# Attention steps with gates: the second bank of transposes goes from VectorE to ScalarE

## The chip, the cores and the metric

The kernel runs on one core of one Trainium2 chip. The metric is the device time of one execution in microseconds (us), lower is better. The engines meant below are TensorE (PE, with its weight loads PEld), VectorE (DVE), ScalarE (ACT), GpSimd (POOL) and SyncE (SP).

## The reference

Two transformer blocks in float32 work on 512 tokens of width 1024. The first block is a SwiGLU layer, a mixing layer and another SwiGLU layer; the second has a chunked attention, a latent attention and two convolutional SwiGLU layers. The change sits in the mixing layer of the first block. Its heads come in two kinds of eight. The first kind is attention over a band of 128 tokens with a sink. The second kind adds up three attentions, each scaled by a gate of its own:

```
o_cmp, o_sel = nsa_cmp_sel(q_b, k_c, v_c, k_s, v_s, tbl_b)
o_win = banded_attention(q_b, k_w, v_w, tbl_b, WINDOW_B, None)
o_b = gates[:, :, 0] * o_cmp + gates[:, :, 1] * o_sel + gates[:, :, 2] * o_win
```

With 512 tokens all eight blocks of 64 are selected, and a window of 512 covers everything, so that o_sel and o_win are both plain causal attentions over all tokens, with different keys and values. o_cmp attends to 31 compressed keys.

## The kernel before

**Groups and steps.** The mixing layer's attention is one object, att_1, of class PairAttention. It works on two heads at a time. First come 8 steps of the banded kind (four groups of two, given a sink). Then come four groups of the mixed kind, numbered 0 to 3 here, of five steps each. Steps A and B are o_sel and steps C and D are o_win: A and C handle the token blocks 3 and 0, B and D the blocks 2 and 1, each for two heads, so a step has four units. Step W handles the compressed keys. A, B, C and D are given a gate. The units of A and C are 512, 512, 128 and 128 keys wide, those of B and D 384, 384, 256 and 256. This makes 16 steps with a gate.

**What one step needs.** TensorE makes the scores (L1810). VectorE adds the bias and takes the row minimum, one instruction per unit (L1974). ScalarE takes the exponential with its row sum, one per unit (L1906). VectorE inverts the sums, of units 0 and 1 at L1948 and of units 2 and 3 at L1961. The probabilities are scaled by inverse and gate (L2033), unit 0 on VectorE and the others on GpSimd. TensorE transposes them in tiles of 128x128 (L1832) into up to three PSUM banks: the first holds unit 0, the second unit 1, and the third units 2 and 3, which is 512, 512 and 256 columns for A and C and 384, 384 and 512 for B and D. The banks are copied into score in SBUF, by ScalarE at L1919 or by VectorE at L1921. TensorE multiplies them with the values (L1857), units 0 and 1 first, and units 2 and 3 as soon as the third bank is copied. When a group's last step is through, ScalarE and VectorE take the result out (L1894, L1899).

**Order by hand.** Every engine has its own order, written as a loop over k, the step whose scores are made. With lag 2, the pass of the loop for step k also handles step k-2's transposes and copies, and step k-3's values. Within mixed groups the pass for A copies the D before, B copies W, C copies A, D copies B, and W copies C. TensorE's pass is scores of k, values of k-3, transposes of k-2. ScalarE's pass is in the function act below. VectorE's pass, beyond what is printed at the end of this section, is in short:

```
self.biased_dve(dve, k)
...
dve.wait_ge(self.e, self.after("e", k, 2))
dve.reciprocal(self.inverses(k, 0, 2), self.sums(k, 0, 2)).then_inc(self.r, 1)
...
self.copies(dve, copied, "dve")
...
self.scaled_dve(dve, k, 1)
...
dve.wait_ge(self.e, self.after("e", k))
```

The last wait is for all four exponentials of step k; the second inversion follows, and then the next pass begins with biased_dve of step k+1. For W the pass is different: L1990 to L1997 prepare it, ScalarE takes its exponential last in its own pass (L1890), and VectorE then takes its sums (L2002 to L2006). In groups 1 and 2 VectorE also splits half a chunk of a later weight in that pass (L2345). After W of group 3 there are no more scores, and TensorE fills the passes with pieces of the output projection (L351 to L353).

Of the kernel before, what the change touches and what calls it, by code (L numbers as in the profile page):

```python
# [87 lines left out]
def program(nc, A, strips_dram, skewed, rows_dram, out):  # L88
    stack = ExitStack()
    with stack:  # L90
# [229 lines left out]
        def split_hi(act, c, slot, land, n=CHUNK):  # L320
            act.wait_ge(raw_landed[slot], land)
            if not isinstance(c, int) or c > 3:
                act.wait_ge(used, c - 2)
            act.activation(w_hi[:, slot, :n], raw[:, slot, :n], ACT.Copy).then_inc(hi_done, 1)  # L324
# [190 lines left out]
        def root_table(act):  # L515

            act.wait_ge(lo_done, 2)
            act.activation(stat[:, 0:1], eps[:, :], ACT.Sqrt)

        def c_row_act(act):  # L520
            act.wait_ge(cond_in, 16)
            act.activation(c_row[:, :], c_row[:, :], ACT.Silu).then_inc(cond_done, 1)
# [56 lines left out]
        class Norm:  # L579
            parts = 1  # L580

            def __init__(self, ready, gains=None, shifts=None, first=0, again=False, tile=xn_tile, banks=None):
                self.tile = tile
                self.n, self.ready, self.gains, self.shifts, self.again = TOK * norms[0], ready, gains, shifts, again
                norms[0] += 1
                self.root_n = TOK * roots[0]
                if not again:
                    roots[0] += 1
                self.first = first
                self.banks = banks or [bank[(t + first) % KT] for t in range(KT)]  # L590
                if gains is not None:
                    self.t, self.e = transposed[0], evacuated[0]
                    transposed[0] += KT
                    evacuated[0] += self.parts * KT
                if shifts is not None:
                    self.f = shifted[0]
                    shifted[0] += self.parts * KT // 2
# [16 lines left out]
            def act(self, act, gained=None, between=None):  # L614

                if not self.again:
                    for s in range(TOK):
                        self.stats_act(act, s)
                if between:
                    between(act)  # L620
                if gained is not None:
                    act.wait_ge(*gained)
                self.evacuate_act(act, range(KT))
# [1062 lines left out]
        class Step:  # L1686


            def __init__(self, units, sink=None, gate=None):
                self.units, self.sink, self.gate, self.windows = units, sink, gate, None  # L1690
                self.banks, width = [], SEQ + 1
                for i, unit in enumerate(units):
                    if width + unit.n > SEQ:
                        self.banks.append([])
                        width = 0
                    unit.bank, unit.col = len(self.banks) - 1, width
                    self.banks[-1].append(i)
                    width += unit.n
                self.copies = ["act", "dve", "act"][:len(self.banks)]
                self.by_dve = [i for i in range(4) if i in SCALED_BY_DVE]  # L1700
                self.by_pool = [i for i in range(4) if i not in SCALED_BY_DVE]
                self.counts = dict(s=4, b=4, e=4, r=2 if sink is None else 1, n=len(self.by_pool), nd=len(self.by_dve), t=len(self.banks),
                                   pa=self.copies.count("act"), pd=self.copies.count("dve"), o=2)
# [4 lines left out]
        class Windows:  # L1708


            def __init__(self, p):
                self.windows, self.sink, self.copies = p, None, ["act"]
                self.counts = dict(s=2, b=1, e=1, r=1, n=1, nd=0, t=1, pa=1, pd=0, o=2)

        pair_link = Count(sem("pair_link"))
# [1 line left out]
        class PairAttention:  # L1717
# [146 lines left out]
            def act(self, act, beside={}):  # L1864
                lag = self.lag
                for k in range(len(self.steps) + lag + 1):
                    if k in beside:
                        beside[k](act)
                    step = self.steps[k] if k < len(self.steps) else None
                    out_of, copied = k - lag - 1, k - lag  # L1870
                    early = out_of in self.last and self.steps[out_of].windows is not None
                    if early:
                        self.out_act(act, out_of)
                    if step and step.windows is None:
                        self.exps_act(act, k, (0, 1))
                    if out_of in self.last and not early:
                        self.out_act(act, out_of)
                    if 0 <= copied < len(self.steps):
                        self.copies(act, copied, "act", (0,))
                    if step and step.windows is None:  # L1880
                        self.exps_act(act, k, (2, 3))
                    if step and step.sink is not None:
                        act.wait_ge(self.sink_d, self.sinks_to(k))
                        at = 16 + 4 * (k % 2)
                        act.activation(stat[:, at:at + 4], stat[:, at:at + 4], ACT.Exp).then_inc(self.sink_e, 1)
                    if 0 <= copied < len(self.steps):
                        self.copies(act, copied, "act", (1, 2))
                    if step and step.windows is not None:
                        act.wait_ge(self.apart, self.windows_to(k))
                        act.activation(self.window_probs(k), self.window_probs(k), ACT.Exp, scale=-1.0).then_inc(self.e, 1)  # L1890
# [1336 lines left out]
```

## Time and profile before

| | |
|---|---|
| median of 3 runs | 2224.39 us (2224.09 to 2224.95) |
| profiled execution, its own time | 2223.66 us |
| span of the profiled execution | 2222.1 us |
| busy: PE, PEld | 2176.4 us (98%), 1816.4 us (82%) |
| busy: DVE, ACT, POOL | 1275.6 us (57%), 898.9 us (40%), 267.4 us (12%) |
| mixed groups, first bias to last values of W | 523.3 to 612.3 us of the span |

Busy time is the time in which an engine executed instructions. The granted clock is the share of TensorE's full speed that it was allowed. In a timeline, a row has its start in us from the beginning of the span, its length, the engine, the line of the kernel, the operation and its tiles, and in brackets how long the engine sat idle before it and who ended that. Consecutive rows overlap a little, because an instruction starts before the one ahead of it has left the engine.

### The profile page before, as it was taken

The page shows a single profiled execution, that of the slowest core. Times are in us where ns is not written, and L with a number is a line of the kernel's source. Part 1 is how long each engine was busy: PE and PEld are TensorE (multiplying, and loading weights), DVE is VectorE, ACT ScalarE, POOL GpSimd, SP SyncE. Part 2 cuts the span into 40 slices and gives each one's busy share as a digit, 9 for nine tenths or more (in the row PEclk, how much of TensorE's full clock was granted, in tenths as well). Part 3 has the DMA queues.
Part 4 walks back from the last instruction along what each step waited for, and adds up shares of the span by engine and source line. Part 5 has one row for each costly group of instructions (what it writes and reads, how often), then busy time and mean ns, then how long its engine had stood idle before and what let it go on. Part 6 is the DMA issues. An engine that isn't in the chain of part 4 may idle for free.

```text
span 2222.1 us, 30869 instructions
## 1 busy us (share of the span) xinstructions
PE 2176.4 (98%) x11681; PEld 1816.4 (82%) x11681; DVE 1275.6 (57%) x2136; ACT 898.9 (40%) x1492; POOL 267.4 (12%) x445
## 2 busy tenths in 40 slices
PE   7999999998999999999999999999999999999998
PEld 6888888877888888888888888888878788888887
DVE  5764764557753363365347766456476766555654
ACT  4222223456642222225237544234264745432343
POOL 2110220045300020010027000000000430000000
PEclk9999999999999999999999999999999999999999
DMA  8864993231034284274231342332313112323332
GB/s 263 285 207 125 320 304 103 95 88 39 30 114 114 76 273 142 66 246 143 95 105 41 91 110 79 105 100 80 114 50 102 61 48 80 100 86 104 94 93 96
DMA packets 260212, 270.42 MB, mean 122 GB/s; under 512 B 9190, under 2 KB 202365, under 8 KB 260109
## 3 DMA queue, kind: packets, MB, share of 16 engines
q1 hardware_dynamic: 238381, 190.40, 28.8%
q0 software_dynamic: 21728, 78.63, 10.2%
q8 instruction: 66, 1.08, 0.2%
q14 instruction: 37, 0.30, 0.0%
HBM read 265.72 MB, written 12.72 MB: 125 GB/s over the span
## 4 chain that ended last, share of the span: by engine, by line
PE 85%; DVE 6%; ACT 5%; issue 1%; POOL 1%; DMA 1%; SPq 0%; DVEq 0%; ACTq 0%; POOLq 0%
PE bank L345 16%; PE bank L346 16%; PE bank L347 15%; PE bank L351 11%; PE bank L353 11%; PE bank L352 11%; PE bank L1857 2%; PE bank L1832 2%; PE bank L1810 2%; ACT probs L1906 1%; DVE w_lo L328 1%; ACT w_hi L324 1%; POOL probs L2032 1%; DVE probs L1974 1%; ACT xT_hi L773 1%
## 5 line engine op out<-in xcount | busy, mean ns | idle before, releaser
L345 PE MATMUL bank<-xT_hi,w_hi 128*128 128x512 f32 (+1 forms) x1624 | 620.3, 382 | 7.0 <-DVE xT_lo L789 2.3
L346 PE MATMUL bank<-xT_lo,w_hi 128*128 128x512 f32 (+1 forms) x1624 | 618.3, 381 | 0.0
L347 PE MATMUL bank<-xT_hi,w_lo 128*128 128x512 f32 (+1 forms) x1624 | 618.2, 381 | 0.0
L328 DVE TENSOR_TENSOR w_lo<-raw,w_hi 128x2048 fp32r<-128x2048 f32 (+2 forms) x200 | 411.0, 2055 | 316.8 <-ACT w_hi L324 315.1
L324 ACT ACTIVATE w_hi<-raw 128x2048 fp32r<-128x2048 f32 (+3 forms) x201 | 345.9, 1721 | 453.5 <-PE bank L353 396.2
L345 PEld LDWEIGHTS bank<-xT_hi,w_hi 128*128 128x128 f32 x1624 | 304.6, 188 | 69.1 <-DVE w_lo L328 5.4
L347 PEld LDWEIGHTS bank<-xT_hi,w_lo 128*128 128x128 f32 x1624 | 304.6, 188 | 59.2
L346 PEld LDWEIGHTS bank<-xT_lo,w_hi 128*128 128x128 f32 x1624 | 304.6, 188 | 58.0
L351 PE MATMUL bank<-w_hi,hid_hi 128*128 128x512 f32 x704 | 274.1, 389 | 0.0
L353 PE MATMUL bank<-w_hi,hid_lo 128*128 128x512 f32 x704 | 273.9, 389 | 0.0
L352 PE MATMUL bank<-w_lo,hid_hi 128*128 128x512 f32 x704 | 273.9, 389 | 0.0
L2032 POOL TENSOR_SCALAR probs<-probs,small 128x256 f32<-128x256 f32 (+2 forms) x120 | 113.8, 960 | 692.4 <-DVE small L1948 673.5
L1027 ACT ACTIVATE hid_hi<-act_u 128x512 f32 (+1 forms) x88 | 55.6, 632 | 310.2 <-DVE act_u L1103 310.2
L353 PEld LDWEIGHTS bank<-w_hi,hid_lo 128*128 128x128 f32 x704 | 132.2, 188 | 27.7
L351 PEld LDWEIGHTS bank<-w_hi,hid_hi 128*128 128x128 f32 x704 | 132.2, 188 | 27.2
L352 PEld LDWEIGHTS bank<-w_lo,hid_hi 128*128 128x128 f32 x704 | 132.2, 188 | 27.2
L1906 ACT ACTIVATE probs<-probs,small 128x512 f32<-128x512 f32 (+2 forms) x224 | 120.8, 542 | 48.8 <-DVE small L1974 48.8
L1095 DVE SCALAR_TENSOR_TENSOR act_u<-bank,cols,act_u 128x511 f32<-128x511 f32 x88 | 65.9, 749 | 94.1 <-ACT act_u L1019 89.0
L1019 ACT ACTIVATE act_u<-bank,cols 128x512 f32<-128x512 f32 x44 | 34.3, 780 | 178.2 <-PE bank L347 178.2
L351 PE MATMUL bank<-w_hi,xT_hi 128*128 128x512 f32 (+2 forms) x288 | 101.8, 354 | 3.3 <-DVE xT_lo L789 2.4
L1106 DVE TENSOR_TENSOR hid_lo<-act_u,hid_hi 128x512 f32 (+1 forms) x88 | 60.9, 693 | 75.4 <-ACT hid_hi L1027 75.4
L352 PE MATMUL bank<-w_lo,xT_hi 128*128 128x512 f32 (+2 forms) x288 | 100.1, 348 | 0.0
(330 smaller groups left out, 2754.6 us busy)
## 6 DMA issues: line engine op xcount, KB each, us to landing
raw<-in_ffn_w_in_dram SPq DMA_DIRECT2D x40, 1024.0 KB, 6.2
raw<-in_f_win_dram SPq DMA_DIRECT2D x40, 1024.0 KB, 6.0
mod_w<-in_mod_w_dram POOLq DMA_DIRECT2D x48, 512.0 KB, 5.9
mod_w_more<-in_mod_w_dram POOLq DMA_DIRECT2D x48, 512.0 KB, 6.1
raw<-in_ffn_w_out_dram SPq DMA_DIRECT2D x24, 768.0 KB, 4.6
raw<-in_f_wout_dram SPq DMA_DIRECT2D x24, 768.0 KB, 4.5
raw<-in_a_wqkv_dram SPq DMA_DIRECT2D x12, 1024.0 KB, 5.1
skewed_strips<-bias_strips POOLq DMA_DIRECT2D x32, 320.0 KB, 6.8
```

What stands on the lines that cost most here:

```text
L324: act.activation(w_hi[:, slot, :n], raw[:, slot, :n], ACT.Copy).then_inc(hi_done, 1)
L328: dve.tensor_tensor(out=w_lo[:, slot, :n], in0=raw[:, slot, :n], in1=w_hi[:, slot, :n].bitcast(f32), op=ALU.subtract).then_inc(lo_done, 1)
L345: pe.matmul(o, lhsT=w[0], rhs=xs[0], start=first, stop=False)
L346: pe.matmul(o, lhsT=w[0], rhs=xs[1], start=False, stop=False)
L347: return pe.matmul(o, lhsT=w[1], rhs=xs[0], start=False, stop=last)
L351: pe.matmul(o, lhsT=xs[0], rhs=w[0], start=first, stop=False)
L352: pe.matmul(o, lhsT=xs[0], rhs=w[1], start=False, stop=False)
L353: return pe.matmul(o, lhsT=xs[1], rhs=w[0], start=False, stop=last)
L1095: dve.scalar_tensor_tensor(out=dst[:, u, shift:], in0=bank[b][:, :SEQ - shift], scalar=w, in1=dst[:, u, shift:], op0=ALU.mult, op1=ALU.add ...
L1106: dve.tensor_tensor(out=hid[1], in0=act_u[:, u, :], in1=hid[0].bitcast(f32), op=ALU.subtract).then_inc(pair_free[u], 1)
L1906: act.activation(p, p, ACT.Exp, scale=-1.0, bias=self.least(k, i), accum_out=self.sums(k, i)).then_inc(self.e, 1)
L2032: return engine.tensor_scalar(p, p, self.inverses(k, i), None, ALU.mult)
```

## The change

In steps that have a gate, the second bank (unit 1's) is copied by ScalarE directly behind the first one, and no longer by VectorE. The other steps are as before.

```
-                self.copies = ["act", "dve", "act"][:len(self.banks)]
+                self.copies = ["act", "dve" if gate is None else "act", "act"][:len(self.banks)]
...
-                self.windows, self.sink, self.copies = p, None, ["act"]
+                self.windows, self.sink, self.gate, self.copies = p, None, None, ["act"]
...
                     if 0 <= copied < len(self.steps):
-                        self.copies(act, copied, "act", (0,))
+                        self.copies(act, copied, "act", (0,) if self.steps[copied].gate is None else (0, 1))
...
                     if 0 <= copied < len(self.steps):
-                        self.copies(act, copied, "act", (1, 2))
+                        self.copies(act, copied, "act", (1, 2) if self.steps[copied].gate is None else (2,))
```

The function copied, by which TensorE waits for banks, reads the same list, so it now waits for ScalarE's count alone in these steps.

## Rows read from the trace of the kernel before

**Rows 1.** Copies out of PSUM, whole run: count, then nanoseconds min/median/max, and forms.

```profile
L1919 ACT ACTIVATE score<-bank x108: 360/573/599, 494.2 to 1807.3; 128x512 f32<-128x512 f32 x56, 128x256 f32<-128x256 f32 x28, 128x384 f32<-128x384 f32 x24
...
L1921 DVE COPY score<-bank x56: 418/614/693, 494.3 to 1806.8; 128x512 f32<-128x512 f32 x28, 128x384 f32<-128x384 f32 x24, 128x256 f32<-128x256 f32 x4
```

**Rows 2.** Group 2: us, busy PE, PEld, DVE, ACT, POOL (instructions), clock, DMA, GB/s.

```profile
563.89:582.17 18.28, 17.53 (x214) 14.86 (x210) 16.15 (x58) 13.66 (x43) 8.37 (x17) 1.00 0.03 3
```

**Rows 3.** Chain that ended last, 515 to 640 us, its shares by line.

```profile
by line: ACT probs L1906 14.3%; DVE probs L1974 8.8%; PE bank L351 8.6%; PE bank L352 8.2%; PE bank L1857 8.2%; PE bank L353 8.2%; PE bank L1832 7.0%; issue 5.3%; DVE score L1921 4.9%; PE bank L2146 4.7%; ACT w_hi L324 3.0%; DVE q_lo L1899 
```

**Rows 4.** Timeline of ScalarE in group 2.

```profile
564.76 0.72 ACT L1906 ACTIVATE probs<-probs,small 128x512 f32<-128x512 f32 x1 [1.78 <-DVE small L1974]
...
566.18 0.47 ACT L1919 ACTIVATE score<-bank 128x384 f32<-128x384 f32 x1
566.55 0.39 ACT L1906 ACTIVATE probs<-probs,small 128x128 f32<-128x128 f32 x1
...
567.33 0.57 ACT L1919 ACTIVATE score<-bank 128x512 f32<-128x512 f32 x1
...
571.24 0.60 ACT L1894 ACTIVATE q_hi<-bank 128x512 fp32r<-128x512 f32 x1 [0.42 <-PE bank L2155]
...
573.15 0.58 ACT L1919 ACTIVATE score<-bank 128x512 f32<-128x512 f32 x1
573.63 0.39 ACT L1906 ACTIVATE probs<-probs,small 128x128 f32<-128x128 f32 x1
...
574.30 0.19 ACT L1906 ACTIVATION_READ_ACCUMULATOR probs<-probs,small 128x1 f32 x1
...
577.82 0.58 ACT L1919 ACTIVATE score<-bank 128x512 f32<-128x512 f32 x1
580.01 1.04 ACT L1919 ACTIVATE score<-bank 128x512 f32<-128x512 f32 x2 [1.61 <-PE bank L1832]
580.95 0.41 ACT L1890 ACTIVATE probs<-probs 128x256 f32<-128x256 f32 x1
```

**Rows 5.** Timeline of VectorE in group 2.

```profile
574.53 0.17 DVE L1961 RECIPROCAL small<-stat 128x2 f32<-128x2 f32 x1
...
577.95 0.17 DVE L1961 RECIPROCAL small<-stat 128x2 f32<-128x2 f32 x1 [0.22 <-ACT probs L1906]
...
581.39 0.42 DVE L2002 TENSOR_REDUCE stat<-probs 128x8 f32<-128x256 f32 x1
```

**Rows 6.** Timeline of TensorE in group 2, the values.

```profile
567.09 1.52 PE L1857 MATMUL bank<-score,v_tok 128*64 128x128 f32 x20
...
574.15 1.31 PE L1857 MATMUL bank<-score,v_tok 128*64 128x128 f32 x20 [0.65 <-DVE score L1921]
...
578.08 1.31 PE L1857 MATMUL bank<-score,v_tok 128*64 128x128 f32 x20
```

**Rows 7.** Timeline of ScalarE, then TensorE, in group 0.

```profile
540.97 0.58 ACT L1919 ACTIVATE score<-bank 128x512 f32<-128x512 f32 x1
543.32 1.04 ACT L1919 ACTIVATE score<-bank 128x512 f32<-128x512 f32 x2 [1.78 <-PE bank L1832]
544.25 0.41 ACT L1890 ACTIVATE probs<-probs 128x256 f32<-128x256 f32 x1
...
541.38 1.31 PE L1857 MATMUL bank<-score,v_tok 128*64 128x128 f32 x20
```

**Rows 8.** Timeline of TensorE behind group 3's last scores.

```profile
601.63 1.31 PE L1857 MATMUL bank<-score,v_tok 128*64 128x128 f32 x20
```

**Rows 9.** Who waited for whom, 523 to 612 us: total, times, longest.

```profile
PE bank L1857 <- DVE score L1921: 2.0, 3, 0.7
```

**Rows 10.** Stretches of 4 us, columns as in the second group.

```profile
508.00:512.00 4.00, 2.93 (x30) 2.45 (x31) 3.47 (x13) 0.95 (x6) 2.43 (x3) 1.00 0.00 0
512.00:516.00 4.00, 3.82 (x34) 3.12 (x32) 3.13 (x16) 3.15 (x13) 2.55 (x4) 0.66 0.42 131
...
572.00:576.00 4.00, 3.35 (x42) 2.84 (x41) 4.00 (x18) 3.52 (x13) 1.86 (x4) 1.00 0.01 2
```

## The prediction, made before the changed kernel was run

> **What bounds the kernel now.** I read the page first: TensorE is busy 98% of the span, so nearly everywhere else a shift of the other engines is free. The question is whether it is free where the change works, between 523 and 612 us. Next I read the chain that ended last over that stretch [rows 3]. TensorE does not own it there: ScalarE's exponentials, VectorE's biases and VectorE's copy (L1921, 4.9%) are on it. Then one mixed group by itself [rows 2]. A group takes 18.28 us (group 1 takes the same to the hundredth). VectorE is busy 16.15 of it, ScalarE 13.66, and TensorE 17.53. So three engines are each near their limit, and the order within the passes decides. Last came the timelines of group 2, engine by engine [rows 4 to 6].
>
> The reader should see a loop there. A bias on VectorE releases the exponentials of units 0 and 1 on ScalarE (the 1.78 us of idle time in [rows 4] end so); a copy sits between them and the exponentials of units 2 and 3; these release VectorE's second inversion; only behind it does the next step's bias run. Whatever ScalarE does between the two pairs of exponentials lengthens this loop. VectorE's copy, in contrast, runs beside the second pair of exponentials: in the pass for C, ScalarE's last exponential, whose sum is read out until 574.49 [rows 4], is done when VectorE with its copy and its scaling is done too, and the second inversion starts at 574.53 [rows 5].
>
> **The change by parts.** *Removed from VectorE:* 16 copies, 8 of 512 columns and 8 of 384, out of the 56 in [rows 1]. Their median is 0.61 us, so 2.5 us a group. Most are hidden beside the exponentials, as just said, so I count no gain for them in the loop. One gain could be in the pass for C, where TensorE waits 0.65 us for VectorE's copy before the values [rows 6], three times in all [rows 9]. But ScalarE's copy 0 starts at 573.15 and the next instruction follows at 573.63 [rows 4]; a copy 1 started there takes 0.58 and ends at 574.21, when TensorE, at 574.15, had already begun behind VectorE's. No gain there either.
>
> *Added to ScalarE:* the same 16 copies. The price of one is how much later the next instruction starts: 0.48 us for 512 columns (573.15 to 573.63) and 0.37 for 384 (566.18 to 566.55) [rows 4]. Back to back they should cost the same. Fourteen of them are ahead of the point where TensorE becomes the only bound (7 of each width); the last two, of C and D of group 3, fall between pieces of the projection, where TensorE has no idle time ahead of the values [rows 8], and cost nothing. If that cover failed, they would cost 0.85 more.
>
> *What is late next,* for one full group that starts with ScalarE and VectorE late by s, times of group 2:
> 1. Pass A copies D, 384 columns: the second exponentials and the third copy are 0.37 later. TensorE already waits for this third copy: its values at 567.09 take 1.52 us and not 1.31 [rows 6]. Six tenths of these values (those of units 0 and 1; 0.74 us of 1.24, which is 1.31 less the overlap with the next row) come before that bank, so the rest started at 567.09 + 0.74 + 0.21 = 568.04, which is 0.71 behind the third copy's start at 567.33. I use this 0.71 again. TensorE is late by s + 0.37.
> 2. Pass B copies W and is unchanged. At its end ScalarE waits 0.42 for TensorE's values of W before L1894 [rows 4], so it takes over TensorE's lateness, s + 0.37.
> 3. Pass C copies A, 512 columns: + 0.48. The inversion at 574.53 had no slack on ScalarE's side. Late: s + 0.85.
> 4. Pass D copies B, 384 columns: + 0.37, and the inversion at 577.95 was already waiting for ScalarE [rows 5]. Late: s + 1.22. The third copy moves from 577.82 to 579.04 + s, and the values of units 2 and 3 can start at 579.75 + s. They would have started at 578.08 + 0.74 = 578.82 [rows 6]. TensorE is late by s + 0.93; a slack of 0.29 is used up.
> 5. Pass W copies C. Before, copy 0 at 580.01, then a wait for the last transpose, copy 2, and L1890 at 580.95, 0.94 later [rows 4]. Now three copies back to back, 0.48 + 0.48 + 0.37 = 1.33, so L1890 and with it L2002 [rows 5] and the next group's bias are 0.39 later than TensorE: s + 1.32.
>
> So a full group adds 1.32 us. Group 0 begins undisturbed at its pass C: 0.48 + 0.37 = 0.85; the third copy at 540.97 then releases the values at 542.53, against 541.38 + 0.74 = 542.12 [rows 7], so TensorE is late by 0.41; L1890 then by 0.41 + 0.40 = 0.81. Groups 1 and 2 add 1.32 each: 3.45. Group 3 counts only up to the values of B, 0.93: 4.38. From there on TensorE is busy with pieces of the projection, and nothing later is changed, so the lateness reaches the end.
>
> Bounds: a copy costs nothing if ScalarE's idle time takes it, and at most its whole length, 0.58 or 0.47, if back to back copies do not overlap: 7 x 0.58 + 7 x 0.47 = 7.4 us. I take the steps of 0.48 and 0.37, since a copy is followed like that by another instruction in [rows 4]. *Moved waits:* the copy's wait for the transposes now holds up ScalarE's second exponentials, but the transposes of k-2 ended long before, except in pass W, which is item 5. TensorE has one wait fewer per step, worth hundredths.
>
> The profiled execution would go from 2223.66 to 2228.04 us; the median of the runs lies 0.73 above it, which makes 2228.8.
>
> **A rule that speaks for the change.** By [rows 2] VectorE is the busier of the two. The Trainium skill (Perfetto Trace Analysis, Identifying the Most-Contended Engine) says to find the vector or scalar engine with the highest occupancy and optimize that one first. By that rule, relieving VectorE should help, as in the third rival below.
>
> **Rivals.**
> - *Everything on the path.* No slack is found: all 14 copies at their steps, 7 x 0.48 + 7 x 0.37 = 5.95 us, 2230.3. For it: the loop has very little idle time. Against: the slacks in items 4 and 5 are in the rows.
> - *The clock falls.* More idle time of TensorE in passes A and C takes its clock down. In [rows 10] a stretch with 2.93 us busy of 4 is followed by one at 0.66; the one with 3.35, which holds the gap at 574.15, kept 1.00. That gap grows from 0.65 to about 0.8, so I expect 3.1 to 3.2 in the worst stretch, between the two. A fall would cost 4 x 0.34 = 1.4 us, once in each of three groups 4.1: 2232.9. [...]
> - *VectorE's relief pays* (not slower). ScalarE has 4.6 us of idle time in a group [rows 2], and if its copy came early enough the three waits of [rows 9] vanish: 2224.4 - 2.0 = 2222.4. It needs ScalarE's copy 1 to end before about 573.4, and its copy 0 alone ends at 573.73. At the extreme the whole share of L1921 leaves the chain [rows 3], 4.9% of 125 us = 6.1: 2218.3.
> - *Partly absorbed.* ScalarE's waits for VectorE and TensorE take half of it, because VectorE, 2.5 us a group less busy, is back sooner: 0 to 2.5 us, middle 2225.7. Against: VectorE's passes end on ScalarE's last exponential, not on its own work.
>
> That the change does not take effect is excluded by the code: the list of copies rules both engines and TensorE's waits.
>
> **How the numbers follow.** A measurement of this kernel tells about 0.2%, 4.45 us, from no change; that line is at 2228.84, and my forecast is almost on it. Chances: the forecast (3.0 to 5.5 us, 2227.4 to 2229.9) 0.60, split evenly by the line; all on the path 0.12 and the clock 0.07, both slower; partly absorbed 0.14 and the small gain 0.04, both within; the large gain 0.03. So slower 0.49, within 0.48, faster 0.03. The range of 2225.3 to 2230.9 leaves out the gains, the clock and about a third of the absorbed case, 0.19.
>
> **What would show it.** L1919 has 124 instructions and L1921 40. A full group takes 19.6 us and not 18.28, with ScalarE busy about 15.7 and VectorE 13.7 in it. In pass C the second inversion waits for ScalarE by some 0.4 us. L1921 is gone from the chain and L1919 is in it. TensorE's values of B wait for L1919 in every group. The projection's piece behind group 3's transposes starts 4.4 us later. The prediction is wrong if a group's length is 18.5 or less (then VectorE's release found a way into the loop that I have missed), if the clock falls, or if stages behind 640 us change their lengths.

## The result and the profile after

The changed kernel took 2229.11 us, the median of 18 runs (2226.54 to 2231.33), against 2224.51 of the kernel before (18 runs beside them, 2222.23 to 2226.72): a ratio of 1.0020, with a 95% interval of 1.0013 to 1.0026. That is 4.6 us slower, just over the line of 0.2% that the text before put at 4.45 us. A second measurement gave 2229.28 against 2224.11, a ratio of 1.0023 (1.0013 to 1.0034). The forecast was 2228.8.

The profiled execution took 2229.2 us, with a span of 2227.7, 5.6 longer than before. I split this span by one marker that all kernels have, ScalarE's L1894, which takes a group's result out. From its start in group 0's pass C to its start behind group 3 is "the stretch". It was 612.37 - 535.82 = 76.55 us before and 616.02 - 535.40 = 80.62 after: 4.07 more. Ahead of it, where nothing is changed yet, the start lies 0.42 earlier, and behind it 1.95 were lost (2227.7 - 616.02 = 1611.68 against 1609.73).

First the copies, one line of the kernel each, over the whole changed run. The counts are those expected, 124 and 40, to be held against [rows 1].

```profile
L1919 ACT ACTIVATE score<-bank x124: 362/574/598, 493.8 to 1812.6; 128x512 f32<-128x512 f32 x64, 128x384 f32<-128x384 f32 x32, 128x256 f32<-128x256 f32 x28
...
L1921 DVE COPY score<-bank x40: 417/614/692, 493.9 to 1812.2; 128x512 f32<-128x512 f32 x20, 128x384 f32<-128x384 f32 x16, 128x256 f32<-128x256 f32 x4
```

Then group 2 as a stretch, with the columns of [rows 2], and two stretches of 4 us in it in which TensorE worked little; the second is the least of the group.

```profile
564.55:584.10 19.55, 18.04 (x212) 14.86 (x210) 14.09 (x53) 15.26 (x47) 9.11 (x17) 1.00 0.00 1
...
568.00:572.00 4.00, 3.33 (x40) 2.36 (x40) 2.99 (x12) 3.73 (x15) 2.31 (x4) 1.00 0.00 0
...
574.00:578.00 4.00, 3.23 (x40) 2.51 (x39) 2.92 (x15) 3.52 (x12) 1.92 (x3) 1.00 0.00 0
```

The group takes 19.55 us where it took 18.28. ScalarE is busier and VectorE less busy, as meant, and now ScalarE is the busier of the two. The clock stays whole.

The chain that ended last, from 515 to 640 us, against [rows 3]: VectorE's copy is gone, and ScalarE's exponentials have 22% where they had 14%, and its copies 13.5% where the lines shown did not have them.

```profile
by line: ACT probs L1906 22.2%; ACT score L1919 13.5%; PE bank L351 7.6%; PE bank L352 7.3%; PE bank L353 7.2%; issue 6.9%; PE bank L1857 5.7%; DVE probs L1974 5.0%; PE bank L2155 3.4%; PE bank L1832 3.4%; ACT w_hi L324 3.0%; PE bank L1810 
```

Now the timelines of group 2: ScalarE, then VectorE, then TensorE. Their rows answer to [rows 4 to 6].

```profile
566.21 0.72 ACT L1906 ACTIVATE probs<-probs,small 128x512 f32<-128x512 f32 x1 [1.68 <-DVE small L1974]
...
567.63 0.85 ACT L1919 ACTIVATE score<-bank 128x384 f32<-128x384 f32 x2
568.37 0.39 ACT L1906 ACTIVATE probs<-probs,small 128x128 f32<-128x128 f32 x1
...
573.07 0.60 ACT L1894 ACTIVATE q_hi<-bank 128x512 fp32r<-128x512 f32 x1 [0.51 <-PE bank L2155]
...
574.97 1.07 ACT L1919 ACTIVATE score<-bank 128x512 f32<-128x512 f32 x2
575.93 0.41 ACT L1906 ACTIVATE probs<-probs,small 128x128 f32<-128x128 f32 x1
...
580.50 0.58 ACT L1919 ACTIVATE score<-bank 128x512 f32<-128x512 f32 x1
...
582.41 1.36 ACT L1919 ACTIVATE score<-bank 128x512 f32<-128x512 f32 x3 [1.33 <-PE bank L1832]
583.64 0.43 ACT L1890 ACTIVATE probs<-probs 128x256 f32<-128x256 f32 x1
```

```profile
576.84 0.17 DVE L1961 RECIPROCAL small<-stat 128x2 f32<-128x2 f32 x1 [0.98 <-ACT probs L1906]
...
580.63 0.17 DVE L1961 RECIPROCAL small<-stat 128x2 f32<-128x2 f32 x1 [1.05 <-ACT probs L1906]
...
584.10 0.42 DVE L2002 TENSOR_REDUCE stat<-probs 128x8 f32<-128x256 f32 x1 [0.72 <-ACT probs L1890]
```

```profile
568.53 0.88 PE L1857 MATMUL bank<-score,v_tok 128*64 128x128 f32 x12 [0.30 <-ACT score L1919]
569.78 0.66 PE L1857 MATMUL bank<-score,v_tok 128*64 128x128 f32 x8 [0.37 <-ACT score L1919]
...
576.10 1.47 PE L1857 MATMUL bank<-score,v_tok 128*64 128x128 f32 x20 [0.77 <-ACT score L1919]
...
580.18 1.60 PE L1857 MATMUL bank<-score,v_tok 128*64 128x128 f32 x20
```

The reader should see three things. A pair of copies takes 0.74 us (567.63 to 568.37) or 0.96 (574.97 to 575.93), twice the step of one. VectorE now idles about 1 us ahead of each second inversion in passes C and D, until ScalarE's last exponential: it waits for the time that its copy took, and for ScalarE's delay on top. And TensorE waits for L1919 in pass C, where it waited for L1921, and in pass A, where no wait of its own stood ahead of these values before (567.09 in [rows 6]).

### The profile page after: what moved, and what is told of

The parts are those of the page before. It is cut to its first block, busy times and chain, and to the rows that moved or that the text cites. A ratio compares the mean times of both kernels' runs of the same rounds, so it can differ in the third digit from the quotient of the medians.

```text
span 2227.7 us, 30841 instructions
## 1 busy us (share of the span) xinstructions
PE 2180.6 (98%) x11681; PEld 1818.7 (82%) x11681; DVE 1267.2 (57%) x2120; ACT 905.2 (41%) x1508; POOL 269.7 (12%) x445
## 4 chain that ended last, share of the span: by engine, by line
PE 85%; ACT 6%; DVE 5%; issue 1%; POOL 1%; DMA 1%; SPq 0%; DVEq 0%; ACTq 0%; POOLq 0%
PE bank L345 16%; PE bank L347 15%; PE bank L346 15%; PE bank L351 11%; PE bank L353 11%; PE bank L352 11%; PE bank L1810 2%; PE bank L1857 2%; ACT probs L1906 2%; PE bank L1832 2%; DVE w_lo L328 1%; ACT w_hi L324 1%; POOL probs L2032 1%; ACT score L1919 1%; ACT xT_hi L773 1%
## 5 line engine op out<-in xcount | busy, mean ns | idle before, releaser
L328 DVE TENSOR_TENSOR w_lo<-raw,w_hi 128x2048 fp32r<-128x2048 f32 (+2 forms) x200 | 411.0, 2055 | 315.5 <-ACT w_hi L324 313.6
L324 ACT ACTIVATE w_hi<-raw 128x2048 fp32r<-128x2048 f32 (+3 forms) x201 | 345.9, 1721 | 453.0 <-PE bank L353 398.2
```

The source lines that it names most:

```text
L328: dve.tensor_tensor(out=w_lo[:, slot, :n], in0=raw[:, slot, :n], in1=w_hi[:, slot, :n].bitcast(f32), op=ALU.subtract).then_inc(lo_done, 1)
```

## The experiments

For each kernel there is the length of a full group, from the L1894 in one group's pass C to that in the next group's (groups 1 and 2; by this marker they are 18.38 and 18.29 before, not 18.28), the stretch, what lies behind the stretch, and the ratio of its time to the kernel before, run beside it.

| kernel | groups 1, 2 | stretch | behind | ratio (95%) |
|---|---|---|---|---|
| before | 18.38, 18.29 | 76.55 | 1609.7 | |
| after | 19.54, 19.55 | 80.62 | 1611.7 | 1.0020 (1.0013 to 1.0026) |
| added work only (e1) | 19.56, 19.54 | 80.66 | 1609.9 | 1.0019 (1.0009 to 1.0028) |
| relief only (e2) | 18.08, 18.08 | 75.62 | 1611.6 | 1.0001 (0.9991 to 1.0010) |
| copy behind the exponentials (e3) | 20.03, 20.03 | 82.37 | 1610.0 | 1.0028 (1.0017 to 1.0040) |
| B and D only (e4) | 18.90, 18.86 | 78.10 | 1610.0 | 1.0017 (1.0008 to 1.0027) |
| A and C only (e5) | 18.88, 18.90 | 78.34 | 1610.0 | 1.0013 (1.0004 to 1.0022) |
| W's exponential first (e6) | 18.39, 18.21 | 76.18 | 1609.9 | 0.9998 (0.9989 to 1.0007) |
| the same, C by ScalarE (e7) | 18.02, 18.01 | 76.16 | 1609.9 | 0.9999 (0.9990 to 1.0008) |
| and A's copies first (e8) | 17.88, 17.87 | 75.50 | 1609.8 | 0.9999 (0.9990 to 1.0008) |
| after, again (e9) | 19.55, 19.56 | 80.67 | 1611.6 | 1.0023 (1.0013 to 1.0034) |
| before, again (e10) | 18.39, 18.30 | 76.80 | 1609.8 | 0.9997 (0.9987 to 1.0007) |

The runs of one kernel scatter over some 4 us, so the times alone can't tell the small ones apart. The lengths of groups 1 and 2 repeat to 0.02 us between two profiles of a kernel (e9 and e10), and the verdicts on the mechanism rest on them. The stretch repeats only to 0.25: group 0's part of it took 17.04 us in the first profile of the kernel before and 17.30 in the second.

**e1: the added work without the relief.**

```
+                        if b == 0 and getattr(step, "gate", None) is not None:
+                            if extra.n:
+                                engine.wait_ge(extra.sem, extra.n)
+                            extra.inc(engine.activation(score[:, 3, 0:n], bank[4 + b][:, 0:n], ACT.Copy))
                         engine.activation(score[:, b, 0:n], bank[4 + b][:, 0:n], ACT.Copy).then_inc(self.pa, 1)
```

(on the kernel before; VectorE's copies stay)

> VectorE keeps its copy of the second bank, as in the kernel before, and ScalarE copies the first bank of every gated step one more time, into a spare row that nothing reads. So ScalarE's added work is there and VectorE's relief is not. Theory (the loop): what costs is that a further copy stands between ScalarE's two pairs of exponentials, and VectorE's relief is worth nothing. Then a full mixed group takes 19.5 to 19.6 us, as in the changed kernel (19.54), and the time is 4 to 5 us over before. Rival (the relief pays back a part): without it a group takes clearly longer, by up to the 0.65 us of TensorE's wait for VectorE's copy, 19.8 to 20.2 us, and the time is 5.5 to 7 us over before.

A group took 19.56 and 19.54 us, the changed kernel's 19.54 and 19.55, and the time was 4.35 us over before. So giving VectorE its 2.5 us a group back bought nothing once the copy stood on ScalarE. The rival, that a part comes back, is out.

**e2: the relief without the added work** (it leaves the second bank's copy out).

```
-                self.copies = ["act", "dve", "act"][:len(self.banks)]
+                self.copies = ["act", "dve" if gate is None else "none", "act"][:len(self.banks)]
```

> Nobody copies the second bank in gated steps: the 16 copies are left out, and the values are multiplied with what stood in that row before. So this is VectorE's relief alone. Theory (the loop): the only gain is in pass C, where TensorE then waits for ScalarE's first copy instead of VectorE's; 0.3 us a group, so a full group takes 17.9 to 18.1 us and the time is about 1 us under before. Rival (VectorE is the most occupied engine and its relief counts in full): the group falls to TensorE's own work, 17.6 us, and the time falls by 2 to 6 us.

A group took 18.08 us, within what the loop gives and far from 17.6, and 0.2 to 0.3 less than before. TensorE's wait in pass C shrank from 0.65 to 0.29, and ended with ScalarE's copy:

```profile
572.57 1.47 PE L1857 MATMUL bank<-score,v_tok 128*64 128x128 f32 x20 [0.29 <-ACT score L1919]
```

The stretch was 0.93 shorter. The time was expected about 1 us under before and did not move (2223.83 against 2223.70); in the profile this kernel lost 1.8 us behind the stretch (see e9 and e10).

**e3: the same work on ScalarE, in another place.**

```
-                        self.copies(act, copied, "act", (0,) if self.steps[copied].gate is None else (0, 1))
+                        self.copies(act, copied, "act", (0,))
...
-                        self.copies(act, copied, "act", (1, 2) if self.steps[copied].gate is None else (2,))
+                        self.copies(act, copied, "act", (1, 2))
```

(on the changed kernel)

> As the changed kernel, but ScalarE makes the copy of the second bank behind its second pair of exponentials and not before it. ScalarE's work is the same. Theory (order decides, not the amount): the loop with VectorE is as short as before, but TensorE's values, which need this bank first, now wait for it; 0.6 us in pass A and 0.9 in pass C, and 0.3 for the third copy of pass W, so a full group takes about 20.1 us and the time is 5.5 to 7 us over before. Rival 1 (the amount of ScalarE's work decides): 19.5 us a group, 4 to 5 us over before, as in the changed kernel. Rival 2 (only the wait in the loop with VectorE costs): 18.4 to 18.8 us a group, 0.5 to 2 us over before.

20.03 us a group: with the same instructions on every engine, 0.48 more than the changed kernel. The time was 6.4 us over before, where 5.5 to 7 were expected. This settles that the order counts, and not ScalarE's sum of work alone. ScalarE's exponentials are together again here, but TensorE pays more in pass C:

```profile
578.44 1.31 PE L1857 MATMUL bank<-score,v_tok 128*64 128x128 f32 x20 [1.53 <-ACT score L1919]
```

Rival 2, that only the wait in the loop with VectorE costs, is out as well: TensorE's values are the second thing that a late copy holds up.

**e4 and e5: one half of the steps each.**

```
+                self.early = gate is not None and units[0].n == 384
+                self.copies = ["act", "act" if self.early else "dve", "act"][:len(self.banks)]
...
+                        self.copies(act, copied, "act", (0, 1) if self.steps[copied].early else (0,))
...
+                        self.copies(act, copied, "act", (2,) if self.steps[copied].early else (1, 2))
```

(e4; in e5 the width is 512)

> Only the steps with blocks 2 and 1 (B and D, 384 columns) have their second bank copied by ScalarE; A and C keep VectorE. Theory (the loop, with slacks): pass A makes TensorE and then all engines 0.37 us late, pass D adds 0.37 of which 0.15 to 0.29 is slack, so a full group takes 18.85 to 18.95 us and the time is about 2 us over before. Rival (price by columns: 768 of the 1792 moved in a group): 43% of the 1.26 us that a group got longer, 18.82 us; or nearly nothing, 18.3 to 18.5, if the whole cost is in passes C and W.

> The other half: only A and C (512 columns) have their second bank copied by ScalarE, B and D keep VectorE. Theory (the loop, with slacks): pass A adds nothing, pass C adds 0.48 us, of which 0.29 is slack at the values of B, and pass W adds 0.29 (three copies ran in 1.23 us in the changed kernel and two in 0.94), so a full group takes about 18.75 us, less than the 18.88 of the half with B and D although it moves more columns, and the time is 1 to 2.5 us over before. Rival (price by columns, 1024 of the 1792 moved in a group): 57% of 1.26 us, 19.0 us a group.

e4 came out as expected by its groups, 18.90 and 18.86, but a price by columns gives 18.82, which is too close for a verdict. Its time was 3.15 us over before, where about 2 were expected and the stretch has 1.55. e5 took 18.88 and 18.90, where I had 18.75 and the rival 19.0; it hits neither. By the same marker before and after, e4 costs 0.52 and 0.57 us in groups 1 and 2, and e5 0.50 and 0.61. Two halves with 768 and 1024 columns that cost the same speak against a price by columns. What I was short of in group 2 lies mainly in pass C. There the values of A are held up twice, first for the second bank and then for the third. In e5's group 2 ScalarE starts pass A at 566.22, so the group's own lateness is 1.46 against [rows 4]. The values of A start at 575.74 and take 1.47 us, not 1.31, against 574.15 in [rows 6]: 1.59 + 0.16 - 1.46 = 0.29. TensorE carries this into pass W, and not the 0.19 that the slack would leave (0.48 - 0.29). With pass W's 0.29 that makes 0.58, and group 2 has 18.90 - 18.29 = 0.61:

```profile
575.74 1.47 PE L1858 MATMUL bank<-score,v_tok 128*64 128x128 f32 x20 [0.78 <-ACT score L1920]
```

**e6, e7, e8: can the copy be had for nothing?** In e6 ScalarE takes W's exponential before the copies of C, and nothing is moved between engines. In e7 C's second bank goes to ScalarE as well. In e8 pass C also begins with the copies of A.

```
+                    if step and step.windows is not None:
+                        act.wait_ge(self.apart, self.windows_to(k))
+                        act.activation(self.window_probs(k), self.window_probs(k), ACT.Exp, scale=-1.0).then_inc(self.e, 1)
                     if out_of in self.last and not early:
                         self.out_act(act, out_of)
```

(e6, taken away from the end of the pass; e7 adds, for C alone:)

```
+            def both_by_act(self):
+                self.early, self.copies = True, ["act", "act", "act"]
+                self.counts.update(pa=3, pd=0)
...
+                        self.copies(act, copied, "act", (0, 1) if self.steps[copied].early else (0,))
...
+                        self.copies(act, copied, "act", (2,) if self.steps[copied].early else (1, 2))
...
+            steps[2].both_by_act()
```

(and e8:)

```
                     if early:
                         self.out_act(act, out_of)
+                        if copied < len(self.steps):
+                            self.copies(act, copied, "act", (0,))
...
+                    if early and copied < len(self.steps):
+                        self.copies(dve, copied, "dve")
                     if large:
                         dve.wait_ge(self.e, self.after("e", k, 2))
...
```

> The kernel before with one change of order: in pass W ScalarE takes the exponential of the compressed keys first and makes the copies of C behind it, while VectorE keeps its copies. Theory (VectorE ends pass W in groups 1 and 2, with its split L2345 and its copy, and ScalarE in groups 0 and 3): groups 1 and 2 stay at 18.28 us, the pass W of group 0 is 0.3 to 0.5 us shorter, and the time is unchanged within 0.1%. Rival (ScalarE's exponential ends pass W everywhere): every group is 0.4 us or more shorter, 17.9 us, and the time is 1 to 2 us under before.

> As the previous one, and ScalarE also copies the second bank of C, the one step in five where this copy falls into pass W, behind the exponential and between no pair. Theory (a copy on ScalarE costs only where it stands between exponentials that VectorE waits for): here it costs nothing and takes 0.6 us from VectorE's end of pass W; the next group's bias is 0.56 us earlier, TensorE's wait for the third copy in pass A (0.21) goes away, and the rest is kept by the chain in pass C from TensorE's values of W to its values of A; a full group takes 18.0 to 18.1 us and the time is 0.3 to 1 us under before, within 0.1%. Rival (ScalarE's work costs wherever it is): 18.5 us a group or more, time 1 us or more over before.

> As the previous one, and in pass C the first copy of A is made before ScalarE's exponentials and the second, by VectorE, before its inversion. Theory (TensorE waits in pass C for a chain in which these two copies stand last): both are ready when VectorE's L1899 and copy are through, so the wait of 0.65 us shrinks to about 0.45, ScalarE's sum of work up to its second exponentials is the same, and a full group takes 17.8 to 18.0 us. The time is 0.5 to 1.5 us under before. Rival (the first exponentials, 0.48 us later, hold up GpSimd and VectorE, and with them the transposes): 18.1 us or more.

e6 is as expected for groups 1 and 2: W's exponential starts at 579.67 and not at 580.95, and it buys next to nothing, since VectorE ends the pass with its own copy. Its pass W of group 0 was expected 0.3 to 0.5 us shorter. That part can't be judged: from L1894 in group 0 to L1894 in group 1 it took 16.75 us, and the kernel before took 17.04 and 17.30 in its two profiles. e7 takes 18.02 a group, 0.3 less than before, with one copy in four moved to ScalarE. Its pass W shows why the move is free there. The exponential and the three copies stand after a long wait of ScalarE, and VectorE goes from its split straight on to its sums:

```profile
581.71 0.42 ACT L1884 ACTIVATE probs<-probs 128x256 f32<-128x256 f32 x1 [1.31 <-DVE probs L2003]
582.04 1.34 ACT L1925 ACTIVATE score<-bank 128x512 f32<-128x512 f32 x3
```

```profile
581.60 1.22 DVE L2352 TENSOR_TENSOR w_lo<-raw,w_hi 128x1024 fp32r<-128x1024 f32 x1
582.73 0.41 DVE L2008 TENSOR_REDUCE stat<-probs 128x8 f32<-128x256 f32 x1
```

e8 takes 17.87, with TensorE's wait in pass C at 0.41, and its stretch is 1.05 us shorter than before. Its time, 2223.92 against 2224.95 by the medians, can't be told from no change. None of the three is a proven gain in time; e8 has the shortest stretch of all kernels that do the whole work.

**e9 and e10: the two kernels again,** without an edit, for the 1.95 us behind the stretch.

> The changed kernel once more, for a second profile. In the first one the attention's stretch explains 4.07 us of the 5.6 us between the two spans, and two falls of TensorE's clock behind the attention, at 622 and at 1643 us, go with the rest. Theory (the falls are by chance and not part of the change): the stretch from the first to the last L1894 of the mixed groups takes 80.6 us again, while the falls are gone or at other places, and the span changes by 1 to 2 us with them. Rival (the change brings them on): both falls are there again, at the same places, and what follows the attention again takes 1611.7 us.

> The kernel before once more, for a second profile. Theory (falls by chance): the stretch takes 76.5 us again; a fall behind the attention may now be in this kernel's profile too. Rival (only changed kernels have them): none, and what follows the attention takes 1609.7 us again.

My theory here fell. In the changed kernel's second profile both falls of the clock are back, at the same places, and what lies behind the stretch again takes 1611.6 us. The kernel before again has neither of the two. Here is the stretch behind the attention: before, then after.

```profile
618.00:622.00 4.00, 4.00 (x19) 3.30 (x18) 2.26 (x2) 0.00 (x0) 0.53 (x1) 1.00 0.92 327
622.00:626.00 4.00, 4.00 (x20) 3.30 (x19) 1.00 (x2) 0.00 (x0) 0.00 (x0) 1.00 1.05 396
```

```profile
618.00:622.00 4.00, 2.09 (x9) 1.42 (x9) 3.36 (x2) 2.33 (x2) 1.93 (x4) 1.00 0.49 154
622.00:626.00 4.00, 4.00 (x12) 3.10 (x12) 1.92 (x2) 0.00 (x0) 0.24 (x1) 0.57 0.98 347
```

Both kernels make TensorE wait there for a new chunk of weights (L324, L328), the changed one 3.64 us later in the span, and equally long. TensorE's first matmul behind the wait, before and then after:

```profile
617.16 0.50 PE L351 MATMUL bank<-w_hi,q_hi 128*128 128x512 f32 x1 [1.92 <-DVE w_lo L328]
```

```profile
620.80 0.50 PE L351 MATMUL bank<-w_hi,q_hi 128*128 128x512 f32 x1 [1.91 <-DVE w_lo L328]
```

In the changed one TensorE is busy for only 2.09 us of the 4 from 618, and the next 4 us are at a mean of 0.57 of the clock, mostly at the lower level of 1.2 GHz, with 12 matmuls and not 20. At full clock the work of these 4 us would have taken 4 x 0.43 = 1.7 us less, an estimate from the second row. The fall is not a matter of the copies as such, though, nor of a later wait. e1 has the same stretch to 0.04 us and takes out its last result 0.9 later; TensorE waits 1.92 us there too, and yet it has no fall and needs 1609.9. e2, whose copies only became fewer, has one: at 0.70 in the second row below, and behind its stretch it needs 1611.6.

```profile
610.00:614.00 4.00, 3.60 (x25) 2.59 (x20) 1.52 (x2) 2.71 (x3) 0.59 (x1) 1.00 0.00 0
614.00:618.00 4.00, 2.48 (x6) 2.00 (x7) 3.76 (x2) 1.61 (x1) 1.58 (x3) 0.70 0.78 241
618.00:622.00 4.00, 4.00 (x17) 3.20 (x17) 0.69 (x1) 0.00 (x0) 0.00 (x0) 0.87 1.04 395
```

Take the piece from the stretch's end to TensorE's next L744, near 645 us. It is 33.70 to 33.76 us long in the three profiles with a fall in it (after, e2, e9) and 32.12 to 32.17 in the nine without, and TensorE's wait in it is 1.91 to 1.92 in all twelve. So a fall goes with 1.6 us, and the fall does not follow from the length of the wait. What comes behind L744 takes 1577.6 to 1577.9 us in all twelve: 1.6 of the 1.95 us are the fall, and the remaining 0.3 is no more than profiles differ by. What puts the fall in one kernel and not in another is not shown. The changed kernel's second fall, near 1643 us, has its like in e6, e7 and e8 4 to 6 us earlier, and there it goes with nothing: they need 1609.8 to 1609.9. This is e8's, at 0.72:

```profile
1636.00:1642.00 6.00, 5.67 (x31) 5.40 (x32) 5.78 (x14) 5.67 (x18) 0.00 (x0) 0.72 0.00 1
```

What of it is in the timed runs stays open. The mean granted clock of each run is on record. It is 0.995 in both profiled executions of the changed kernel and in one other of its 27 runs, while 15 of them have 0.998 and average 2228.8 us; the runs of the kernel before have mostly 0.997. So in most of the changed kernel's runs TensorE spent less time at the lower level than in its two profiles, and they were slower than the kernel before all the same; which falls they lacked is not known. The time of e1, without the fall in its profile, is 4.35 us over before, and that of the changed kernel 4.6 and 5.2; these agree within their intervals.

## Why the prediction was right, point by point

**The loop.** Its reading held. e1 has the whole cost with none of the relief, and e3 shows with the same work that the place decides. The forecast of 4.38 us stands against 4.07 in the stretch, and of 19.6 for a group against 19.55. Step by step in group 2, the lateness against the rows of before:

| item | forecast | measured |
|---|---|---|
| at the start of pass A (566.21 - 564.76) | s | 1.45 |
| 1, 2: L1894 | s + 0.37 | 573.07 - 571.24 = 1.83, s + 0.38 |
| 3: second inversion of C | s + 0.85 | 576.84 - 574.53 = 2.31, s + 0.86 |
| 4: second inversion of D | s + 1.22 | 580.63 - 577.95 = 2.68, s + 1.23 |
| 4: TensorE behind the values of B (copy 0 of C) | s + 0.93 | 582.41 - 580.01 = 2.40, s + 0.95 |
| 5: L1890 | s + 1.32 | 583.64 - 580.95 = 2.69, s + 1.24 |

**The term that was mis-sized** is the 1.33 us of three copies back to back in item 5. They took 1.23 (582.41 to 583.64), so pass W adds 0.29 and not 0.39. Over three groups that is the 0.3 us between 4.38 and 4.07. The fault is in the third of the three steps, 0.48 + 0.48 + 0.37. The third bank of C has 256 columns and was priced with the 0.37 of 384. A copy of 256 columns holds ScalarE up by 0.27 us in the kernel before, and by 0.26 in the changed one (583.38 to 583.64): 0.48 + 0.48 + 0.26 = 1.22. First before, then after:

```profile
569.48 0.36 ACT L1919 ACTIVATE score<-bank 128x256 f32<-128x256 f32 x1
569.75 0.49 ACT L1906 ACTIVATE probs<-probs,small 128x256 f32<-128x256 f32 x1
```

```profile
583.38 0.39 ACT L1919 ACTIVATE score<-bank 128x256 f32<-128x256 f32 x1
583.64 0.43 ACT L1890 ACTIVATE probs<-probs 128x256 f32<-128x256 f32 x1
```

The forecast's assumption that copies cost the same back to back was right.

**The signs that the text before gave.** The counts, the group's length and the chain came as said. Three were off. VectorE was busy 14.09 us in a group and not 13.7, and ScalarE 15.26 and not 15.7. The second inversion of pass C waits 0.98 us and not 0.4, because the time that the copy took on VectorE was left out of that figure. And the first piece of the projection behind group 3's transposes starts 3.65 us later and not 4.4, which is the 4.38 less the 0.3 above and the 0.42 that the profile gained ahead.

**The relief at no gain.** Right in the changed kernel (e1), where ScalarE's copy ends no earlier than VectorE's did. By itself the relief is worth 0.2 to 0.3 us a group (e2), which the text before had only as a rival's part. The rule that it weighed, from the Trainium skill (Perfetto Trace Analysis, Identifying the Most-Contended Engine), did not pay here: VectorE was, of the two, the engine with the higher occupancy, its busy time in a group fell by 2.1 us, and the group grew by 1.3. In e2, where nobody takes over the work, the relief bought 0.2 to 0.3.

**The cover of the last two copies** held: from the L1894 that takes out group 2's result to the one for group 3's, the two kernels differ by (616.02 - 592.62) - (612.37 - 589.53) = 0.56 us, all of it in passes C and D ahead of the last values of B.

**The clock.** Inside the attention the worst stretch has 3.23 us busy of 4, where 3.1 to 3.2 were expected, and the clock stayed at 1.00. The forecast sum took what lies behind the attention as unchanged, and in the profiles that was not so: 1.95 us went there, 1.6 of them ahead of 650 us with the fall of the clock. A fall of the clock was among the things that would make the forecast wrong; its price was worked out for falls inside the groups alone, and none came there. Behind 650 us the stages kept their lengths to 0.3 us. The profiled run is at 2229.2, where the forecast had 2228.04; with the stretch's 4.07 alone it would be near 2227.7 (2223.66 + 4.07). So the small distance between forecast and profiled run, 1.2 us, is a sum of things that were not foreseen: 0.3 too much in the loop, 0.42 gained ahead of it and 1.95 lost behind it. That the medians meet to 0.3 us (2228.8 and 2229.11), where runs scatter over 4, is in part luck; the mechanism rests on the group lengths.

**The rivals.** Everything on the path (5.95) and partly absorbed (0 to 2.5) are both off the stretch's 4.07. The slack at the values of B is real: TensorE is late by s + 0.95 there, where the second inversion is late by s + 1.23. So is the one in pass W, where 0.48 of added work costs 0.29. A gain was never near: in e2, with nobody copying the second bank, a group is only 0.2 to 0.3 shorter.

## What to carry to other kernels

When two engines hand work to and fro, ask of each instruction between which two handovers it stands, and not how busy its engine is. The same copy cost its full 0.37 to 0.48 us between two exponentials that the other engine waited for, more than that behind them, where TensorE waited, and nothing in pass W, once it stood behind a wait and behind the exponential. And price a copy by a row of its own width. For a change of a few us, compare the length of one repeated group in the trace: here it repeats to 0.02 us, where whole times scatter over 4.

## What the runs showed of the hardware

- A copy of a PSUM bank by ScalarE takes 0.36 to 0.39, 0.47 or 0.58 us for 256, 384 or 512 columns, but holds up the next instruction by only 0.26 to 0.27, 0.37 or 0.48, whether an exponential or another copy stands behind it. Two together take 0.74 (384 columns) and 0.96 (512), and three (512, 512 and 256 columns) 1.23.
- TensorE's clock can fall in a part that a change does not touch. The same wait of 1.9 us behind the attention was followed by matmuls at the lower level of 1.2 GHz in both profiles of the changed kernel and in e2's, and in none of the other nine. A fall there goes with 1.6 us, and in the profile of e2 it took away a gain. The later fall, near 1640 us, went with nothing in e6, e7 and e8.
